# TensorE sums three of the sixteen rows of the first two modulation units and turns x's tiles between its last sums

## The reference, cut to what matters

```python
cond = jax.nn.silu(c)                                  # (1, 1024)
mod = (cond @ w_ada[l] + b_ada[l]).reshape(b, 9, d)    # nine vectors of 1024 per layer
h = modulate(x, mod[:, 0], mod[:, 1])                  # x * (1 + scale) + shift
x = post_norm_residual(x, swiglu(h, w_ffn_in[l, 0], w_ffn_out[l, 0]), mod[:, 2], 0.5, ...)
```

## Time and profile before

| | |
|---|---|
| median of 3 runs | 1035.95 us (1035.7 to 1037.51) |
| span of the profiled execution, first to last instruction | 1034.2 us |
| that execution's own time | not listed apart from the three runs; the median is 1.75 us above the span |
| PE busy | 1008.3 us (97%) |
| DVE busy | 781.2 us (76%) |
| ACT busy | 524.7 us (51%) |
| bytes moved | 265.62 MB, mean 257 GB/s |
| mean granted TensorE clock | 0.995 |

### The profile page before, as it was taken

How to read it: one execution, slowest core, us unless ns; L and a number is a source line. 1 busy time by engine, 2 the same in 40 slices (tenths; PEclk the granted TensorE clock), 3 DMA queues, 4 the chain that set the end, 5 groups by cost and what they waited for, 6 DMA issues and landing times.

```text
span 1034.2 us, 12480 instructions
## 1 busy us (share of the span) xinstructions
PE 1008.3 (97%) x4768; PEld 832.3 (80%) x4768; DVE 781.2 (76%) x915; ACT 524.7 (51%) x843; POOL 86.0 (8%) x160
## 2 busy tenths in 40 slices
PE   4999999999999999999999999999999999999997
PEld 3878888888888888888878888888888878888885
DVE  6888677879876897768887587777888977545485
ACT  1645453566465753545465644443568764434432
POOL 0011111000000011111000011111010010000000
PEclk9999999999999999999999999999999999999999
DMA  9999899846775499998928499989846748556541
GB/s 352 376 380 379 300 301 312 304 162 225 261 246 163 145 383 342 295 310 304 337 82 304 142 359 300 306 301 308 304 157 217 241 140 298 185 182 202 176 151 41
DMA packets 147491, 265.62 MB, mean 257 GB/s; under 512 B 8424, under 2 KB 98920, under 8 KB 147432
## 3 DMA queue, kind: packets, MB, share of 16 engines
q1 hardware_dynamic: 124448, 182.87, 52.2%
q0 software_dynamic: 20928, 75.53, 20.9%
q10 hardware_dynamic: 2056, 6.42, 1.9%
HBM read 263.75 MB, written 1.05 MB: 256 GB/s over the span
## 4 chain that ended last, share of the span: by engine, by line
PE 82%; DVE 9%; ACT 4%; issue 2%; DMA 2%; SPq 0%; DVEq 0%; ACTq 0%
PE psum L1419 17%; PE psum L1421 17%; PE psum L1420 17%; PE psum L1515 8%; PE psum L1517 8%; PE psum L1516 8%; DVE w_lo L951 2%; DMA raw<-in_w_ffn_in 2%; PE psum L1554 2%; ACT w_hi L584 1%; ACT psum L698 1%; DVE qT L1143 1%; PE psum L1454 1%; DVE qT L1144 1%; DVE tmp L972 1%
## 5 line engine op out<-in xcount | busy, mean ns | idle before, releaser
L951 DVE TENSOR_TENSOR w_lo<-raw,w_hi 128x2048 fp32r<-128x2048 f32 x164 | 371.5, 2286 | 61.2 <-ACT w_hi L584 61.1
L1419 PE MATMUL psum<-w_hi,hT_hi 128*128 128x512 f32 x896 | 355.6, 397 | 0.3
L1421 PE MATMUL psum<-w_hi,hT_lo 128*128 128x512 f32 x896 | 350.0, 391 | 0.0
L1420 PE MATMUL psum<-w_lo,hT_hi 128*128 128x512 f32 x896 | 349.0, 390 | 0.0
L584 ACT ACTIVATE w_hi<-raw 128x2048 fp32r<-128x2048 f32 x164 | 309.4, 1915 | 11.9 <-DMA raw<-in_w_ffn_in 9.6
L590 ACT ACTIVATE tmp<-psum 128x256 f32<-128x256 f32 x88 | 33.6, 383 | 338.4 <-PE psum L1421 338.4
L1421 PEld LDWEIGHTS psum<-w_hi,hT_lo 128*128 128x128 f32 x896 | 168.2, 188 | 35.9
L1419 PEld LDWEIGHTS psum<-w_hi,hT_hi 128*128 128x128 f32 x896 | 168.3, 188 | 35.4 <-issue 2.3
L1420 PEld LDWEIGHTS psum<-w_lo,hT_hi 128*128 128x128 f32 x896 | 168.5, 188 | 33.0
L1515 PE MATMUL psum<-w_hi,a_hi 128*128 128x512 f32 x368 | 147.8, 402 | 0.0
L1517 PE MATMUL psum<-w_hi,a_lo 128*128 128x512 f32 x368 | 143.8, 391 | 0.0
(11 more groups left out here) (166 smaller groups left out, 772.5 us busy)
## 6 DMA issues: line engine op xcount, KB each, us to landing
raw<-in_w_ffn_in SPq DMA_DIRECT2D x176, 512.0 KB, 5.6
raw<-in_w_ffn_out SPq DMA_DIRECT2D x88, 512.0 KB, 6.2
ada<-in_w_ada POOLq DMA_DIRECT2D x72, 512.0 KB, 6.0
qT<-in_w_ada POOLq DMA_DIRECT2D x56, 512.0 KB, 4.8
raw<-in_w_qkv_a SPq DMA_DIRECT2D x24, 512.0 KB, 4.8
raw<-in_w_o SPq DMA_DIRECT2D x16, 512.0 KB, 4.7
raw<-in_w_kv_b SPq DMA_DIRECT2D x16, 512.0 KB, 5.1
raw<-in_w_ada SPq DMA_DIRECT2D x4, 1024.0 KB, 16.3
```

The source lines that it names most:

```text
L951: nc.vector.tensor_tensor(lo_of(n), slot_of(n), hi_of(n).bitcast(F32), ALU.subtract)\
L1419: nc.tensor.matmul(dst, s_hi, m_hi, start=start, stop=False)
L1420: nc.tensor.matmul(dst, s_hi, m_lo, start=False, stop=False)
L1421: return nc.tensor.matmul(dst, s_lo, m_hi, start=False, stop=stop)
```

## The change

TensorE takes three rows from VectorE: both rows of staged tile 3 and the first of tile 6. A new function `sum_row` multiplies a row and its column of cond in one matmul for each 128 columns: the row is the stationary operand, cond's column (128 x 1) the moving one, and the result is added to the same column of `misc` as the sums of the accumulator. The counts that other engines wait for are adjusted, chunks 1 and 4 wait in addition for `tensor_rows_read`, and the products with zeros are 44, 16, 16 and 2 in place of 44, 40 and 8. The second tile of x is turned after the last sums.

```diff
-START_PRODUCTS = (44, 40, 8)
-MORE_STEPS = 1
+START_PRODUCTS = (44, 16, 16, 2)
+TENSOR_ROWS = [(3, 0), (3, 1), (6, 0)]
+MORE_STEPS = 1 - len(TENSOR_ROWS)
...
+def start_steps(m, r):
+    rows = [(a, b) for a in range(STAGED) for b in range(2) if (a, b) not in TENSOR_ROWS]
+    return sum(row < (m, r) for row in rows)
...
-                    sp.wait_ge(acc_steps, 2 * (n + 2) + 2)
+                    sp.wait_ge(acc_steps, start_steps(n + 3, 0))
+                    if n in (1, 4):
+                        sp.wait_ge(tensor_rows_read, (n + 2) // 3)
...
                 for r in range(2):
+                    if (m, r) in TENSOR_ROWS:
+                        continue
...
+            def sum_row(m, r, dst, tiles, first=False):
+                part, factor = staged(m)[:, r, :], cond[:, 2 * (m % 4) + r:2 * (m % 4) + r + 1]
+                for k in tiles:
+                    last = nc.tensor.matmul(dst[:, k:k + 1], part[:, k * P:(k + 1) * P], factor,
+                                            start=first and k == tiles[0], stop=True, skip_group_check=True)
+                return last
...
             stay_busy(START_PRODUCTS[0])
-            pe.wait_ge(acc_steps, 8)
-            sum_start(acc0, misc[0][:, 0:8], range(KT), True)
+            pe.wait_ge(cond_ready, 1)
+            pe.wait_ge(staged_in[3], 16)
+            sum_row(3, 0, misc[0][:, 0:8], range(KT), True)
+            sum_row(3, 1, misc[0][:, 0:8], range(KT)).then_inc(tensor_rows_read, 1)
+            pe.wait_ge(acc_steps, start_steps(4, 0))
+            sum_start(acc0, misc[0][:, 0:8], range(KT))
             stay_busy(START_PRODUCTS[1])
-            pe.wait_ge(acc_steps, 16)
+            pe.wait_ge(staged_in[6], 16)
+            sum_row(6, 0, misc[0][:, 8:16], range(4))
+            sum_row(6, 0, misc[1][:, 8:16], range(4, KT), True).then_inc(tensor_rows_read, 1)
+            stay_busy(START_PRODUCTS[2])
+            pe.wait_ge(acc_steps, MORE_STEPS + 15)
             sum_start(acc, misc[0][:, 8:16], range(4)).then_inc(start_sums, 1)
-            for t in range(TT):
-                pe.wait_ge(x_in[t], 16)
-                turn_x(0, t)
-            pe.wait_ge(acc_steps, 17)
-            sum_start(acc, misc[1][:, 8:16], range(4, KT), True).then_inc(start_sums, 1)
-            stay_busy(START_PRODUCTS[2])
+            pe.wait_ge(x_in[0], 16)
+            turn_x(0, 0)
+            pe.wait_ge(acc_steps, MORE_STEPS + 16)
+            sum_start(acc, misc[1][:, 8:16], range(4, KT)).then_inc(start_sums, 1)
+            pe.wait_ge(x_in[1], 16)
+            turn_x(0, 1)
+            stay_busy(START_PRODUCTS[3])
```

More of the change, by code:

```diff
@@ L293, in build @@
         start_sums = sem("start_sums")
+        tensor_rows_read = sem("tensor_rows_read")
         bias_in = sem("bias_in")
@@ L962, in start_rows @@
                         continue
-                    dve.wait_ge(acc_steps, 2 * m + r)
+                    dve.wait_ge(acc_steps, start_steps(m, r))
                     if (m, r) == (STAGED - 1, 1):
```

## The result

| | launches | median, us | lowest to highest |
|---|---|---|---|
| before | 14 | 1035.92 | 1035.46 to 1037.70 |
| changed | 14 | 1036.76 | 1035.60 to 1041.17 |

The ratio is 1.0022, with a 95% interval of 1.0011 to 1.0032: the change makes the kernel slower, by some 2.3 us on average. The median alone hides how. Six of the fourteen launches of the changed kernel took 1040.8 to 1041.2 us, and the other eight 1035.6 to 1036.8. Of 98 launches of the kernel before that were run beside the experiments none took over 1038.5. Two disturbed launches, one of the kernel before at 4263 us and one of e4 at 1220 us with a mean granted clock of 0.79, are left out throughout.

The account below looks back on a forecast made before the run. The prediction took chunk 6's transfer behind full DMA engines, then TensorE, as the bound; a 1.2 us earlier start would vanish in the wait: 1034.2 + 0 + 1.75 = 1035.9 us, range 1034.0 to 1039.0.

Parts of the forecast that it names:

- The path to the end: Start of the kernel: its gains or losses reach the end only through TensorE's 1.7 us wait at L1554, set by chunk 6.
- the sum: Likeliest case: span 1034.2, effect of the change 0, plus 1.75 to the median, giving 1035.9 us; chance 0.50.
- late return: TensorE's clock falls at about 21.1 and returns late; layer starts at 44.5, kernel 7 to 9 us slower; chance 0.18.
- rival (a): TensorE's clock falls during the one-column sums at the start: slower; chance 0.18 with a late, 0.14 with an early recovery.
- spare 1.7 us: TensorE's wait before L1554 for work behind chunk 6's transfer; a start later by up to 1.7 us was to cost nothing.
- The sum's case: Start with TensorE's clock full throughout: the layer's first matmul at 34.4 instead of 35.61, with no effect on the end.
- early return: TensorE's clock falls but is back after the first 16 products; layer starts at 38.1, costing 0.8 us; chance 0.14.
- VectorE's 2.5 us: Start: with three rows fewer, VectorE has acc's first half at 28.7 instead of 31.2, limited by the last staged row's landing.
- the lead: TensorE reaches L1554 1.2 us earlier and only waits longer, 2.9 us, since chunk 6 still lands at 54.57.
- The added waits of SP: Chunk 1 waits for TensorE's read of tile 3, chunk 4 for tile 6; both were to cost nothing.
- Rival (b): Chunk 6 lands earlier because its 13.52 us is latency behind the issue: 1035.3, at most 1033.4 us; chance 0.14.
- Rival (c): Longer idle time before L1554 makes TensorE's clock fall, 1.5 us lost: 1037.4 us; chance 0.04.

Follow-up runs that it names:

- e4: Kernel before, with POOL's third and fourth row (1 MB) waiting for the split of chunk 5 instead of chunk 2: median 1033.6 us, ratio 0.9971.
- e5: Changed kernel, with POOL's third and fourth row waiting for the split of chunk 5: six launches at 1033.90 to 1034.34 us, six at 1040.71 to 1041.22.
- e12: Changed kernel with its products with zeros as 44, 24, 8, 2 instead of 44, 16, 16, 2: median 1036.31 us, ratio 1.0006 to before.
- e11: Only both rows of tile 3 on TensorE, tile 6 on VectorE, products 44, 32, 4, POOL's rows as before: median 1036.09 us, ratio 1.0002 to before.
- e3: Changed kernel with the 32 products placed one ahead of each one-column matmul of the three rows and acc0's sum: median 1036.65 us.
- e2: Changed kernel with pieces of 8 products where 16 stood (44, 8, 8, 2): median 1037.8 us, ratio 1.0009 to before.
- e1: Changed kernel with its 16 + 16 products in one piece of 32 (44, 32, 0, 2): median 1036.2 us, ratio 1.0001 to before.
- e9: Kernel before, unaltered, run again; its profiled launch, of the slower group, took 1037.48 us.
- e6: Changed kernel, unaltered, run again: five launches at 1035.74 to 1036.24 us, one at 1038.35, six at 1040.61 to 1041.86.
- e10: Kernel before, unaltered, run once more for a profile: 1035.88 us, of the faster group.

## Why the prediction was wrong

It gave 1035.9, "same" with 0.69 and "slower" with 0.19; measured is slower by 0.22% (0.11 to 0.32). The path to the end was right, the transfer of chunk 6 as long as TensorE's start is at most 1.7 us late. What failed is the clock: the sum put its fall at nothing, and the odds of its late return were too low.

**What fails.** The step is rival (a), "Chance of the late return 0.18", and in it the argument against it: "2.65 us of products reached the faster rate, and 16 slow products last longer than that". Going by the times, it happened in 12 of 26 launches. Two profiles with the same 16 products at the same time and pace, one with a return at their end and one without (e5), show that 16 slow products sometimes bring the clock back and sometimes don't; with 24 and with 32 in the first piece no launch was near 1041 (0 of 11 each), and with 8 the one profile has no return before the layer. I had taken one profile's 2.65 us for a sure length. It is among the shortest there are: in the fourteen profiles the same first products reached the faster pace after 2.7 to 5.9 us, 13 to 28 products. The price times the odds comes out as well: at 0.46, five microseconds make 2.3 us on average, which is what the ratio says.

**The size of the late return.** Worked out at 44.5 us for the layer's start and 1043 to 1045 for the time; measured 41.9 and 1040.7. The one-column matmuls were taken at 0.223 us a record at half clock, and the chain has 3.20 / 16 = 0.20 for tile 6's row and 1.50 / 8 = 0.19 for acc: the busy time of a group counts the end of its last matmul. And the clock was back 1.3 us after the layer's own matmuls began (43.2), where I gave them a while. Less the spare 1.7 us, 41.9 - 35.6 - 1.7 = 4.6 us, and the span shows 4.7 (1038.9 against 1034.2).

**The sum's case never occurred in a profile.** "With the clock full throughout" the layer was to start at 34.4. In both profiles of the changed kernel the clock fell, and the layer started at 35.7 and 35.6: the early return, which I had at 38.1 and 0.8 us slower. The pieces were shorter than I gave them: the first products ended at 28.5 instead of 29.8, and from there to the layer it took 7.2 us instead of 8.3, since at full clock the records take 0.11 us (1.78 / 16), not 0.131. So the early return cost nothing that shows. Here the rule of the Trainium skill ("TensorE: Matmul & The Clock Gate", section "Why this matters for your kernels"), to leave TensorE no idle gaps so that the clock stays up, was not enough: from 17.90 to 21.78 there was no gap, and the clock fell.

**VectorE's 2.5 us** were 1.1: the first half of acc came at 29.39 + 0.7 = 30.1, not at 28.7. The landing that it waited for was that of tile 6 (26.68), and behind it stand one row of tile 6 and all of tile 7. But the last row would have allowed no more: it landed at 29.2, where I had 27.95 from the profile before. In e12 tile 6 came early enough, and the halves still began at 29.32. Why the staged tiles land about 1 us later in every profile with rows on TensorE (28.8 to 29.2 for the last, against 27.9 to 28.2) stays open.

**What became of the lead** was right in kind: a start 1.2 us earlier (e11) grew the wait by 0.4 us and moved nothing. The landing of chunk 6 was between 54.2 and 54.8 in the eight profiles with POOL's rows as before in which it was issued between 40.4 and 42.0. Issued at 43.5 (e3), 44.6 (e2) and 44.8 (e1), it landed at 54.9, 54.3 and 55.7. Taking 1 MB from ahead of it moved it 2.9 us (e4). The added waits of SP cost nothing, as said: in the changed kernel SP's first chunk was issued at 21.9 and the DMA share stayed at 1.05. Rival (b) is refuted by the same landings.

**Rival (c)**, the fall behind a longer wait, was given 0.04. It is there already in the kernel before: one profile shows it (e9), and 31 of 98 launches lie where it would put them, at about the price that I gave it, 1.5 us. My reason against it, that before it took more than 3 us without work, came from one profile, of the other group.

## What to carry to other kernels

Work that keeps TensorE's queue full does not by itself keep its clock: one-column matmuls did not, and where the end hangs on the clock's return, the length of the filler has to be chosen from many launches, not from one profile. Here the longer fillers (e1, e12) took away the loss of 5 us, and made the kernel no faster than before. When an average moves by 0.2%, look at the single times before looking for a cause: two groups 5 us apart want another explanation than a shift. And before making work earlier that ends in a wait for a transfer, ask what stands ahead of that transfer: putting 1 MB behind it (e4) brought 0.29%, more than three rows moved to another engine could.

## What the runs showed of the hardware that was not expected

- With one-column matmuls alone and no gap, the granted clock fell 3.6 us (profile after, e6) to 5.0 us (e12) after they began, and it stayed at half through 17 us of unbroken mixed work (e2).
- The same products from 11.6 to 12.0 us on reached the faster pace after 2.7 us (profile before) to 5.9 us (e12).
- A wait of 1.65 us (e9) or 2.1 us (e11), with two transposes between it and the matmuls before, was followed by 3.4 us at half clock. Behind waits of 1.6 to 2.1 us in the same place the clock did not fall in the profiles before, after, e6, e10 and e12. With the wait gone (e4) no group 1.5 us higher is left: 1033.49 to 1034.22 in eight launches. Why one launch falls and the next does not was not tried.
- The landing of a transfer behind full engines hardly depended on its issue: chunk 6, issued at 41.05 before and 3.6 us later in e2, landed at 54.6 and 54.3.
